# Where four accumulated rows are added over the partitions: one-column products at two places, or row products in column groups at one

## The chip, the cores and the metric

One core of a Trainium2 chip runs the kernel. The metric is the device time of one execution in microseconds (us). Everything the kernel reads lies in the device's main memory (HBM) at its start, and the result is written there.

## The reference, cut to what matters

The block works on 256 latent tokens and 256 context tokens of width 2048. A conditioning vector c is turned into six modulation rows of 2048 numbers, two for the mixing layer's input (shift sh1, scale sc1) and four that are used later:

```python
mod = silu(c) @ w_mod + b_mod                       # 2048 x 12288
sh1, sc1, g1, sh2, sc2, g2 = split(mod, 6)
h  = rms_norm(x, norm_mix_pre) * (1 + sc1) + sh1    # also hc from ctx, c_ctx
y  = hybrid_mixer(h, hc, w_in, ...)                 # projections, 4+4 heads, w_up, w_out
x1 = x + g1 * rms_norm(y, norm_mix_post)
h2 = rms_norm(x1, norm_ffn_pre) * (1 + sc2) + sh2
y2 = (silu(h2 @ ffn_w_gate) * (h2 @ ffn_w_up)) @ ffn_w_down
out = x1 + g2 * rms_norm(y2, norm_ffn_post)
```

The change is about the four later rows g1, sh2, sc2 and g2, each a product of the vector silu(c) with a 2048 x 2048 part of `w_mod`.

## The kernel before

All large products stream a weight matrix through TensorE. A **slot** is 256 rows x 512 columns of weights (512 KB). SyncE's queue loads it into one of eight buffers `raw`; ScalarE rounds it to `w_hi` (L593); VectorE makes the rest `w_lo` (L932); TensorE multiplies hi x hi, hi x lo and lo x hi with the activations as stationary operands (L1344, L1348, L1356, function `products`). ScalarE and VectorE may be up to four slots ahead of TensorE. The stages follow one another in one stream of slots: opening, context blocks, latent blocks (`S_LAT`), up (`S_UP`), out (`S_OUT`), feed-forward (`S_FFN`), down (`S_DOWN`). One slot of the latent blocks is 12 products of 512 columns.

**Step numbers.** The smaller work is written out by hand between slots. In the first seven latent blocks, step p stands behind slot p - 4 on TensorE and ahead of the rounding of slot p on ScalarE and VectorE (the three functions `at_pre`; block t, slot j call `at_pre(8t+j+4)` on TensorE and `at_pre(8t+j)` on the two others). So step 37 on TensorE comes after slot 33 and step 46 after slot 42. From block 6 on, `at_head` and `head_pass` do the same for the heads' work.

**The four rows.** In the context blocks and the first latent blocks VectorE adds up `acc[:, g, :] += wm * silu(c)` (L944), where each `wm` is 128 rows of `w_mod`. This leaves for each of the four rows g 128 partial sums, one in each partition, that have still to be added over the partitions. `add_partitions` (L1487) does that with products whose stationary operand is a 128 x 128 piece of `acc` and whose moving operand is one column of ones: 16 fp32 products for one row, each of which the trace shows as two records. The result stands in columns (channel in the partition).

- At step 37 TensorE adds row 0 (g1). VectorE makes the gate's weight from it at step 39 (`gate_weight`, L1043), TensorE turns it into 16 rows of 128 at step 40 (L1497), ScalarE copies it out at step 43 (L756) and GpSimd stores it to `gwd` (L438).
- Rows 1 to 3 wait: GpSimd stores them to memory when the last accumulation is done (`accd`, 3 MB, L420), ahead of the load of the table `dist` (1 MB, L421), and loads them back as `acc2` while w_out's products run (L559).
- At **the bridge** between out and feed-forward, TensorE adds rows 1 to 3 (L1685 to L1688) and then runs `turn_h2` (L1670, products at L1680), which scales and transposes the new residual `hs` into the feed-forward's input; it needs `diag` (L1287), which holds the reciprocal norms. VectorE makes `mod2`, the shift and scale (L1278, L1281), ScalarE applies it (L893, L896), VectorE makes the low part (L1306), and the products of the feed-forward follow pair by pair.
- The gate's weight for g2 is made at L1288, turned after the 11th slot of the first feed-forward block (L1706), copied at L908 and stored at L569.

**GpSimd's order around the change.** L420 and L421 are issued once the last accumulation is done. Then GpSimd works through the decay tables for four heads, three instructions each (L430, L432, L435), which need `dist`; after that it stores `gwd` (L438), adds decays (L442), loads the first head's operands (L446), and turns the first head's queries and keys with the rotary tables (L481 to L485). TensorE needs these at L1565. ScalarE's steps 40, 42, 44 and 46 need one head's decay table each.

## Time and profile before

| | us |
|---|---|
| median of 3 runs | 1807.98 |
| the three runs | 1805.08, 1808.60, 1807.98 |
| the profiled execution, its time | 1805.67 |
| the profiled execution, its span | 1803.7 |
| TensorE busy with matmuls | 1755.7 (97%) |
| VectorE, ScalarE, GpSimd busy | 976.8, 725.6, 163.5 |

The span is what the profile records from the first to the last instruction; the time holds 2 us around it. Times inside the trace are us from the span's start. TensorE's row is busy nearly throughout, which for matmuls that are pipelined does not say that it runs at its peak: a stretch can be full of records and still be slow, because the products are tiny or because the clock granted to TensorE (PEclk, 1.00 is 2.4 GHz and 0.50 is 1.2 GHz) is at the lower level. Columns of each view are explained where its rows stand.

### The profile page before, as it was taken

What the parts mean: (1) busy time and instruction counts of PE and PEld (TensorE: products, weight loads), DVE (VectorE), ACT (ScalarE), POOL (GpSimd) and SP (SyncE); (2) the same over time, 40 slices, a digit from 0 to 9 for tenths busy, and PEclk for the clock granted to TensorE, in tenths of its full rate; (3) what the DMA queues carried; (4) which work ended last, traced back from release to release, by engine and by line L of the source; (5) the groups of instructions that cost most, each with busy time, mean ns of one, the idle gap of its engine ahead of it and who ended that gap; (6) DMA issues with size and microseconds to landing.
All of it is one profiled execution on the core that took longest, in us unless ns stands there. A gap on an engine that the chain in (4) does not pass through costs nothing.

```text
span 1803.7 us, 21863 instructions
## 1 busy us (share of the span) xinstructions
PE 1755.7 (97%) x8012; PEld 1420.2 (79%) x8012; DVE 976.8 (54%) x1036; ACT 725.6 (40%) x797; POOL 163.5 (9%) x177
## 2 busy tenths in 40 slices
PE   5889999999999999999999999999999999999997
PEld 2448888887788888888888898888888888888886
DVE  2327666655676766676565544444444444444444
ACT  3213222224545543554544454444444444443442
POOL 2000000000007452440000000000000000000000
PEclk8999999999999999999999989999999999999999
DMA  8999988886898766665778636666666666766662
GB/s 312 339 362 354 314 306 310 317 292 249 288 335 295 257 183 206 182 191 159 237 227 329 197 118 203 192 187 188 189 191 188 188 189 190 259 189 193 191 192 76
DMA packets 182283, 422.12 MB, mean 234 GB/s; under 512 B 12816, under 2 KB 13120, under 8 KB 171600
## 3 DMA queue, kind: packets, MB, share of 16 engines
q1 hardware_dynamic: 156288, 304.14, 53.2%
q10 hardware_dynamic: 17856, 82.43, 12.5%
q0 software_dynamic: 8080, 34.75, 5.7%
q8 instruction: 39, 0.64, 0.1%
q14 instruction: 20, 0.16, 0.0%
HBM read 397.66 MB, written 23.61 MB: 234 GB/s over the span
## 4 chain that ended last, share of the span: by engine, by line
PE 93%; ACT 2%; DMA 2%; DVE 2%; issue 1%; SPq 0%; POOL 0%; DVEq 0%; ACTq 0%; POOLq 0%
PE ps L1344 28%; PE ps L1348 28%; PE ps L1356 28%; PE ps L1397 2%; DMA raw<-in_w_mod 1%; PE ps L1490 1%; PE ps L1583 1%; DMA xn<-in_x 1%; PE ps L1599 1%; PE ps L1637 1%; ACT w_hi L593 1%; PE ps L1680 0%; PE ps L1469 0%; PE ps L1554 0%; PE ps L1532 0%
## 5 line engine op out<-in xcount | busy, mean ns | idle before, releaser
L932 DVE TENSOR_TENSOR w_lo<-raw,w_hi 128x1024 fp32r<-128x1024 f32 x496 | 617.2, 1248 | 543.9 <-ACT w_hi L593 541.9
L593 ACT ACTIVATE w_hi<-raw 128x1024 fp32r<-128x1024 f32 x496 | 524.3, 1059 | 838.3 <-PE ps L1356 833.8
L1344 PE MATMUL ps<-w_hi,h_hi 128*128 128x512 f32 x1536 | 485.0, 397 | 7.0 <-ACT w_hi L672 7.0
L1348 PE MATMUL ps<-w_hi,h_lo 128*128 128x512 f32 x1536 | 476.5, 391 | 0.0
L1356 PE MATMUL ps<-w_lo,h_hi 128*128 128x512 f32 x1536 | 421.5, 390 | 0.0
L1344 PEld LDWEIGHTS ps<-w_hi,h_hi 128*128 128x128 f32 x1536 | 285.1, 188 | 70.5 <-issue 13.4
L1348 PEld LDWEIGHTS ps<-w_hi,h_lo 128*128 128x128 f32 x1536 | 289.1, 188 | 61.9
L1356 PEld LDWEIGHTS ps<-w_lo,h_hi 128*128 128x128 f32 x1536 | 288.5, 188 | 61.1 <-DVE w_lo L932 0.2
L944 DVE SCALAR_TENSOR_TENSOR acc<-wm,csil,acc 128x2048 f32<-128x2048 f32 (+1 forms) x60 | 141.0, 2350 | 101.0 <-DMA wm<-in_w_mod 100.9
L1348 PE MATMUL ps<-w_hi,hid_lo 128*128 128x512 f32 x352 | 109.4, 392 | 0.0
L1344 PE MATMUL ps<-w_hi,hid_hi 128*128 128x512 f32 x352 | 109.0, 391 | 0.0
L1356 PE MATMUL ps<-w_lo,hid_hi 128*128 128x512 f32 x352 | 94.9, 391 | 0.0
L1356 PEld LDWEIGHTS ps<-w_lo,hid_hi 128*128 128x128 f32 x352 | 66.1, 188 | 14.7
L1344 PEld LDWEIGHTS ps<-w_hi,hid_hi 128*128 128x128 f32 x352 | 66.0, 188 | 14.5
L1348 PEld LDWEIGHTS ps<-w_hi,hid_lo 128*128 128x128 f32 x352 | 66.1, 188 | 14.1
L1348 PE MATMUL ps<-w_hi,hc_lo 128*128 128x512 f32 x224 | 70.4, 396 | 0.0
L1344 PE MATMUL ps<-w_hi,hc_hi 128*128 128x512 f32 x224 | 70.2, 395 | 0.0
L1356 PE MATMUL ps<-w_lo,hc_hi 128*128 128x512 f32 x224 | 69.9, 393 | 0.0
L1397 PE MATMUL ps<-raw,c_pad 128*32 128x512 f32 x256 | 52.3, 636 | 7.3 <-DMA raw<-in_w_mod 6.0
L1348 PEld LDWEIGHTS ps<-w_hi,hc_lo 128*128 128x128 f32 x224 | 42.5, 190 | 10.1
L1344 PEld LDWEIGHTS ps<-w_hi,hc_hi 128*128 128x128 f32 x224 | 42.3, 189 | 9.7
L1356 PEld LDWEIGHTS ps<-w_lo,hc_hi 128*128 128x128 f32 x224 | 42.1, 188 | 9.8
(254 smaller groups left out, 1174.9 us busy)
## 6 DMA issues: line engine op xcount, KB each, us to landing
raw<-in_w_in SPq DMA_DIRECT2D x176, 512.0 KB, 5.5
wm<-in_w_mod ACTq DMA_DIRECT2D x64, 1024.0 KB, 6.9
raw<-in_ffn_w_gate SPq DMA_DIRECT2D x88, 512.0 KB, 4.5
raw<-in_ffn_w_up SPq DMA_DIRECT2D x88, 512.0 KB, 4.4
raw<-in_ffn_w_down SPq DMA_DIRECT2D x88, 512.0 KB, 4.7
raw<-in_w_mod SPq DMA_DIRECT2D x64, 512.0 KB, 8.2
raw<-in_w_out SPq DMA_DIRECT2D x32, 512.0 KB, 5.2
px<-stage ACTq DMA_DIRECT2D x44, 256.0 KB, 6.3
```

Source lines behind the costliest of these rows:

```text
L593: act.activation(w_hi[:, j % SPLIT, :, :], raw[:, j % RAW, :, :], ACT.Copy).then_inc(w_high, 1)
L932: dve.tensor_tensor(w_lo[:, j % SPLIT, :, :], raw[:, j % RAW, :, :], w_hi[:, j % SPLIT, :, :].bitcast(F32), ALU.subtract).then_inc(w_low, 1)
L944: dve.scalar_tensor_tensor(out=a, in0=wm[:, b, :], scalar=csil[:, k:k + 1], in1=a, op0=ALU.mult, op1=ALU.add).then_inc(S("wm_used"), 1)
L1344: pe.matmul(o, hi[:, kk, c], w_hi[:, q, e, :], start=kk == 0, stop=False)
L1348: pe.matmul(o, lo[:, kk, c], w_hi[:, q, e, :], start=False, stop=False)
L1356: last = pe.matmul(o, hi[:, kk, c], w_lo[:, q, e, :], start=False, stop=kk == last_k)
L1397: last = pe.matmul(bank(4 + n % 2)[g * GROUP:(g + 1) * GROUP, :], c_pad[:, k, :], raw[:, place % RAW, e, :], start=k < 3, stop=k >= KT - 3 ...
L1490: last = pe.matmul(dst[:, first + k:first + k + 1], sums[:, g, k * P:(k + 1) * P], ones[:, :], start=True, stop=True)
L1583: last = pe.matmul(bank(4, 2)[:, a * L:(a + 1) * L], r_kt[:, 2 * (a // 2) + f, (a % 2) * P:(a % 2 + 1) * P], r_qt[:, f, :], start=f == 0, ...
L1599: last = pe.matmul(bank(4)[:, m * RDK:(m + 1) * RDK], r_a[:, a, m * P:(m + 1) * P], r_v[:, a, :], start=a == 0, stop=a == 3)
L1637: last = pe.transpose(bank(4, 2)[:, q * L + m * P:q * L + (m + 1) * P], src[:, m, q * P:(q + 1) * P], ident[:, :])
```

## The change

All four rows are added over the partitions at one place, in the latent blocks, with the operands' parts exchanged: the stationary operand is a 128 x 32 block of ones and the moving operand is 512 columns of `acc`. Each such product gives the sums of 512 channels as a row (the same row in 32 partitions). Product c uses the array's column group c mod 3, so that three run side by side. 12 of the 16 stand at step 37 and 4 at step 40. ScalarE copies the rows out at steps 38 and 41; GpSimd stores them to `sumd` (three DMAs, one for each column group, each from one partition), waits, and loads them back as 64 rows of 128 into `rows`; TensorE turns these at step 46; VectorE makes both gate weights and `mod2` at step 47; TensorE turns both gate weights at step 49, ScalarE copies them and GpSimd stores them to `gwd`, now just ahead of the heads' loop. The detour `accd` and `acc2`, the sums at the bridge and the turn in the feed-forward go.

```diff
     gwd = nc.dram_tensor("gwd", (2, D), F32, kind="Internal").ap()
-    accd = nc.dram_tensor("accd", (3, P, D), F32, kind="Internal").ap()
+    sumd = nc.dram_tensor("sumd", (6, 3, N), F32, kind="Internal").ap()
     hsd = nc.dram_tensor("hsd", (L, D), F32, kind="Internal").ap()
...
         ident = keep("ident", [P, P])
-        ones = keep("ones", [P, 1])
+        ones = keep("ones", [P, GROUP])
         rope = keep("rope", [P, 2, MT, P])
...
         gw_cols = keep("gw_cols", [P, 2, KT])
-        gw_rows = keep("gw_rows", [KT, P])
+        gw_rows = keep("gw_rows", [2 * KT, P])
         csil = keep("csil", [P, 2 * KT])
...
         la = reg("la", [P, 2, 4, GH * GDK], 32)
+        sum_row = reg("sum_row", [3 * GROUP, 6, N], 32)
         cum = reg("cum", [P, 2, GH, L + 1], 48)
...
         y = reg("y", [P, MT, D], 52)
-        acc2 = reg("acc2", [P, 3, D], 69)
         hs = reg("hs", [P, MT, D], 0)
...
             pool.wait_ge(S("wm_used"), 4 * KT)
-            pool.dma_start(accd.rearrange("g p n -> p g n"), acc[:, 1:4, :]).then_inc(S("acc_stored"), 16)
             pool.dma_start(dist[:, :, :, :], k_dist).then_inc(S("dist_landed"), 16)
...
                     .then_inc(S("dist_sum"), 1)
-            pool.wait_ge(S("gw_rows_ready"), 1)
-            pool.dma_start(gwd[0].rearrange("(r q) -> r q", q=P), gw_rows[:, :]).then_inc(S("gw_stored"), 16)
+            pool.wait_ge(S("sum_rows_ready"), 2)
+            for g in range(3):
+                pool.dma_start(sumd[:, g:g + 1, :].rearrange("b g n -> g b n"), sum_row[g * GROUP:g * GROUP + 1, :, :])\
+                    .then_inc(S("sums_stored"), 16)
+            pool.wait_ge(S("sums_stored"), 16 * 3)
+            pool.dma_start(rows[0:4 * KT, :], sumd.rearrange("b g (r q) -> (b g r) q", q=P)[0:4 * KT, :])\
+                .then_inc(S("sums_stored"), 16)
...
                 pool.wait_ge(stored[b], 16 * blocks)
-            pool.wait_ge(S("acc_stored"), 16)
             load_g_qk(0)
...
             add_ctx_decay(RH - 1)
+            pool.wait_ge(S("sum_rows_ready"), 3)
+            pool.dma_start(gwd.rearrange("a (r q) -> (a r) q", q=P), gw_rows[:, :]).then_inc(S("gw_stored"), 16)
             pool.wait_ge(S("gw_stored"), 16)
...
             pool.dma_start(g1w[:, :], gwd[0:1, :].broadcast_to([P, D])).then_inc(S("res_landed"), 16)
-            pool.dma_start(acc2[:, :, :], accd.rearrange("g p n -> p g n")).then_inc(S("acc_landed"), 16)
             pool.wait_ge(S("ssy_ready"), 2)
...
-            pool.wait_ge(S("gw_rows_ready"), 2)
-            pool.dma_start(gwd[1].rearrange("(r q) -> r q", q=P), gw_rows[:, :]).then_inc(S("gw_stored"), 16)
-            pool.wait_ge(S("gw_stored"), 32)
             pool.wait_ge(S("hs_stored"), 16 * MT)
...
                                    scale=1.0 / GATE_NORM).then_inc(S("kw_exp"), 1)
-                if p == 43:
-                    act.wait_ge(S("gw_turned"), 1)
-                    act.activation(gw_rows[:, :], bank(5)[0:KT, 0:P], ACT.Copy).then_inc(S("gw_rows_ready"), 1)
+                if p in (38, 41):
+                    r = (p - 38) // 3
+                    act.wait_ge(S("sums_done"), r + 3)
+                    act.activation(sum_row[:, 4 * r:4 + 2 * r, :],
+                                   bank(4, 4 - 2 * r)[0:3 * GROUP, :].rearrange("p (b n) -> p b n", n=N), ACT.Copy)\
+                        .then_inc(S("sum_rows_ready"), 1)
+                if p == 49:
+                    act.wait_ge(S("sums_turned"), 2)
+                    act.activation(gw_rows[:, :], bank(5)[0:2 * KT, 0:P], ACT.Copy).then_inc(S("sum_rows_ready"), 1)
                 if p in (40, 42, 44, 46):
...
                             .then_inc(S("silu_ready"), 1)
-                    if prev is None and j == 15:
-                        act.wait_ge(S("gw_turned"), 2)
-                        act.wait_ge(S("gw_stored"), 16)
-                        act.activation(gw_rows[:, :], bank(6)[0:KT, 0:P], ACT.Copy).then_inc(S("gw_rows_ready"), 1)
                     if prev is not None or j >= 4:
...
                     dve.tensor_tensor(kw[:, d, :, :], kw[:, d, :, :], gkc[:, :, :], ALU.mult).then_inc(S("kw_ready"), 1)
-                if p == 39:
-                    gate_weight(0, bank(4), 1)
-
-            def gate_weight(d, src, done):
-
-                dve.wait_ge(S("partitions_added"), done)
-                dve.tensor_tensor(gw_cols[:, d, :], src[:, 0:KT], cols2[:, 48 * d:48 * d + KT], ALU.add)\
-                    .then_inc(S("mod2_part"), 1)
-                dve.wait_ge(S("mod2_part"), 1 + 4 * d)
-                dve.tensor_tensor(gw_cols[:, d, :], gw_cols[:, d, :], cols2[:, (4 + d) * KT:(5 + d) * KT], ALU.mult)\
-                    .then_inc(S("mod2_part"), 1)
+                if p == 47:
+                    sums = bank(4)[:, 0:4 * KT]
+                    dve.wait_ge(S("sums_turned"), 1)
+                    dve.tensor_tensor(gw_cols[:, 0, :], sums[:, 0:KT], cols2[:, 0:KT], ALU.add).then_inc(S("mod2_part"), 1)
+                    dve.tensor_tensor(gw_cols[:, 1, :], sums[:, 3 * KT:4 * KT], cols2[:, 3 * KT:4 * KT], ALU.add)\
+                        .then_inc(S("mod2_part"), 1)
+                    dve.tensor_tensor(mod2[:, :, :], sums[:, KT:3 * KT].rearrange("p (a k) -> p a k", a=2),
+                                      cols2[:, KT:3 * KT].rearrange("p (a k) -> p a k", a=2), ALU.add)\
+                        .then_inc(S("mod2_part"), 1)
+                    dve.wait_ge(S("mod2_part"), 3)
+                    for d in range(2):
+                        dve.tensor_tensor(gw_cols[:, d, :], gw_cols[:, d, :], cols2[:, (4 + d) * KT:(5 + d) * KT], ALU.mult)\
+                            .then_inc(S("mod2_part"), 1)
+                    dve.scalar_tensor_tensor(out=mod2[:, 1, :], in0=mod2[:, 1, :], scalar=1.0, in1=cols[:, 3 * KT:4 * KT],
+                                             op0=ALU.add, op1=ALU.mult).then_inc(S("mod2_part"), 1)
...
                                          op0=ALU.mult, op1=ALU.add).then_inc(S("hs_ready"), 1)
-            dve.wait_ge(S("partitions_added"), 3)
-            dve.tensor_tensor(mod2[:, :, :], bank(6)[:, 0:2 * KT].rearrange("p (a k) -> p a k", a=2),
-                              cols2[:, KT:3 * KT].rearrange("p (a k) -> p a k", a=2), ALU.add).then_inc(S("mod2_part"), 1)
-            dve.wait_ge(S("mod2_part"), 3)
-            dve.scalar_tensor_tensor(out=mod2[:, 1, :], in0=mod2[:, 1, :], scalar=1.0, in1=cols[:, 3 * KT:4 * KT],
-                                     op0=ALU.add, op1=ALU.mult).then_inc(S("mod2_part"), 1)
             dve.wait_ge(S("square"), 4 + MT)
...
                 dve.tensor_scalar(diag[:, m, :], ident[:, :], rstd[:, 2 + m:3 + m], None, ALU.mult).then_inc(S("diag_ready"), 1)
-            gate_weight(1, bank(7), 4)
...
                     last.then_inc(S("ctx_sums_done"), 1)
-                if p == 37:
-                    pe.wait_ge(S("wm_used"), 4 * KT)
-                    pe.wait_ge(S("kw_exp"), 2)
-                    add_partitions(acc, 0, bank(4), 0)
-                if p == 40:
-                    turn_gate_weight(0, bank(5))
-
-            def add_partitions(sums, g, dst, first):
-
-                for k in range(KT):
-                    last = pe.matmul(dst[:, first + k:first + k + 1], sums[:, g, k * P:(k + 1) * P], ones[:, :],
-                                     start=True, stop=True)
-                last.then_inc(S("partitions_added"), 1)
-
-            def turn_gate_weight(d, dst):
-
-                pe.wait_ge(S("mod2_part"), 2 + 4 * d)
-                pe.transpose(dst[0:KT, 0:P], gw_cols[:, d, :], ident[:, :]).then_inc(S("gw_turned"), 1)
+                if p in (37, 40):
+                    if p == 37:
+                        pe.wait_ge(S("wm_used"), 4 * KT)
+                        pe.wait_ge(S("kw_exp"), 2)
+                    else:
+                        pe.wait_ge(S("sum_rows_ready"), 1)
+                    for c in range(0, 12) if p == 37 else range(12, 16):
+                        g = c % 3
+                        last = pe.matmul(bank(4 + c // 3 % 4)[g * GROUP:(g + 1) * GROUP, :], ones[:, :],
+                                         acc[:, c // 4, c % 4 * N:(c % 4 + 1) * N], start=True, stop=True,
+                                         tile_position=(0, g * GROUP))
+                    last.then_inc(S("sums_done"), 1)
+                if p == 46:
+                    pe.wait_ge(S("sums_stored"), 16 * 4)
+                    pe.wait_ge(S("sum_rows_ready"), 2)
+                    pe.transpose(bank(4)[:, 0:4 * KT], rows[0:4 * KT, :], ident[0:4 * KT, 0:4 * KT])\
+                        .then_inc(S("sums_turned"), 1)
+                if p == 49:
+                    pe.wait_ge(S("mod2_part"), 6)
+                    pe.transpose(bank(5)[0:2 * KT, 0:P], gw_cols[:, :, :].rearrange("p d k -> p (d k)"), ident[:, :])\
+                        .then_inc(S("sums_turned"), 1)
...
                 if t == 6:
-                    pe.wait_ge(S("gw_rows_ready"), 1)
+                    pe.wait_ge(S("sum_rows_ready"), 3)
                 lat_block(S_LAT + 8 * t, 0, t, lambda j: at_head(0, j - 4) if t == 6 and j >= 4 else at_pre(8 * t + j + 4))
...
                     pe.wait_ge(S("diag_ready"), MT)
-                if j == 3:
-                    pe.wait_ge(S("mod2_part"), 5)
                 if j >= 4:
...
-            pe.wait_ge(S("acc_landed"), 16)
-            add_partitions(acc2, 0, bank(6), 0)
-            add_partitions(acc2, 1, bank(6), KT)
-            add_partitions(acc2, 2, bank(7), 0)
             for j in range(3):
...
                             turn_h2(j + 3)
-                        if prev is None and g == 1 and j == 2:
-                            pe.wait_ge(S("h2_hi_ready"), 8)
-                            turn_gate_weight(1, bank(6))
                         if prev is not None and g == 0 and j == 2:
...
             ffn_block(S_FFN, 0, None)
```

## Rows read from the trace of the kernel before

**Rows 1.** The page, part 4: shares of the chain that ended last, by engine.
```profile
PE 93%; ACT 2%; DMA 2%; DVE 2%; issue 1%; SPq 0%; POOL 0%; DVEq 0%; ACTq 0%; POOLq 0%
```

**Rows 2.** Timeline at the bridge: start, length, engine, line, operation, tiles, records [idle before].
```profile
1036.52 15.60 PE L1490 MATMUL ps<-ones,acc 128*128 128x1 f32 x96
...
1048.44 0.48 DVE L1287 TENSOR_SCALAR diag<-ident,rstd 128x128 f32<-128x128 f32 x2 [0.82 <-POOL rstd L566]
...
1051.98 4.61 PE L1680 MATMUL ps<-diag,hs 128*128 128x128 f32 x24
...
1054.08 1.02 ACT L893 ACTIVATE h2f<-ps,mod 128x256 f32<-128x256 f32 x2 [6.67 <-PE ps L1680]
...
1056.58 0.70 PE L1344 MATMUL ps<-w_hi,h_hi 128*128 128x512 f32 x2
```

**Rows 3.** Busy time by stretch, then granted clock, DMA share and GB/s.
```profile
80.00:100.00 20.00, 18.28 (x101) 8.44 (x99) 6.06 (x13) 3.84 (x6) 0.00 (x0) 1.00 0.93 323
543.00:547.20 4.20, 4.20 (x14) 3.33 (x14) 0.00 (x0) 0.00 (x0) 0.00 (x0) 0.59 1.02 411
1044.00:1048.00 4.00, 4.00 (x21) 4.00 (x20) 1.87 (x4) 3.15 (x4) 0.85 (x3) 0.50 0.87 356
1053.50:1056.50 3.00, 3.00 (x19) 2.90 (x18) 0.69 (x1) 2.39 (x5) 0.00 (x0) 0.66 0.00 0
```

**Rows 4.** Timeline of TensorE in the latent blocks, from step 37 on.
```profile
539.51 3.63 PE L1490 MATMUL ps<-ones,acc 128*128 128x1 f32 x32
543.00 0.76 PE L1344 MATMUL ps<-w_hi,h_hi 128*128 128x512 f32 x2
...
547.41 0.61 PE L1344 MATMUL ps<-w_hi,h_hi 128*128 128x512 f32 x2
...
550.13 0.61 PE L1344 MATMUL ps<-w_hi,h_hi 128*128 128x512 f32 x2
...
552.85 0.27 PE L1497 MATMUL ps<-ident,gw_cols 128*16 128x128 f32 x1
...
555.72 0.62 PE L1344 MATMUL ps<-w_hi,h_hi 128*128 128x512 f32 x2
```

**Rows 5.** Timeline of TensorE in the opening: fp32 products in three column groups.
```profile
66.06 1.90 PE L1397 MATMUL ps<-raw,c_pad 128*32 128x512 f32 x8
...
68.88 3.63 PE L1397 MATMUL ps<-raw,c_pad 128*32 128x512 f32 x24
```

**Rows 6.** Timeline of GpSimd (POOL), from the store of acc to the first head.
```profile
532.13 0.75 POOL L420 DMA_DIRECT2D accd<-acc  x1 [34.17 <-DVE acc L944]
532.88 0.57 POOL L421 DMA_DIRECT2D dist<-in_k_dist  x1
...
549.21 2.22 POOL L430 TENSOR_SCALAR d_tmp<-dist,lg 128x512 f32<-128x512 f32 x1 [15.00 <-issue]
...
569.23 1.29 POOL L435 TENSOR_TENSOR dmat<-dmat,d_tmp 128x512 f32<-128x512 f32 x1
...
596.75 1.30 POOL L442 TENSOR_TENSOR dmat<-dmat,d_ctx 128x512 f32<-128x512 f32 x1
...
612.01 1.72 POOL L485 TENSOR_TENSOR r_k<-r_tmp 128x256 f32<-128x256 f32 x1
```

**Rows 7.** DMA queues from 530 to 545 us: packets, MB, share of the 16 engines.
```profile
q0 software_dynamic: 461, 3.65, 65.0%
q1 hardware_dynamic: 572, 1.12, 19.6%
```

**Rows 8.** DMA issues, whole span: times issued, KB each, median us from issue to landing.
```profile
hsd<-hs POOLq DMA_DIRECT2D x2, 1024.0 KB, 4.8
...
g1w<-gwd POOLq DMA_DIRECT2D x1, 1024.0 KB, 13.3
...
gwd<-gw_rows POOLq DMA_DIRECT2D x2, 8.0 KB, 3.4
```

**Rows 9.** Timeline of TensorE where the change's new waits come.
```profile
569.32 0.62 PE L1344 MATMUL ps<-w_hi,h_hi 128*128 128x512 f32 x2
...
617.84 0.60 PE L1565 MATMUL ps<-ident,r_q 128*128 128x128 f32 x4
```

## The prediction

> **What bounds the kernel now.** I read the chain that ended last first: 93% of it is TensorE's own work, so time is won or lost only where TensorE gets or loses microseconds [rows 1]. The second view is the timeline at the two places that the change touches; the reader is to see there what TensorE does while it is "busy". The third is the granted clock of the same stretches, because a stretch full of records can run at half rate. The last are GpSimd's timeline and the DMA views, because the change makes TensorE wait for a chain that runs through GpSimd and memory.
>
> At the bridge TensorE runs 96 records of one-column products for 15.6 us, from 1036.52 to 1052.1, and only then the products that turn the residual (24 records from 1051.98) [rows 2]. What these need besides TensorE, `diag`, is there at 1048.44 + 0.48 = 1048.92 [rows 2]. So the one-column products end the wait last, but by 3 us only; the other 12 of the 15.6 us lie beside the norm of the residual on the other engines, which the change leaves as it is. The big number, 15.6 us removed, isn't the gain.
>
> **The bridge.** Afterwards the turn starts at about 1049.1 (a product follows its last operand by some 0.1 us), against 1051.98: **-2.9**. What is late next is the chain `diag`, turn, ScalarE, VectorE, first product, which is 1056.58 - 1051.98 = 4.6 us long [rows 2] and moves as a whole. The small VectorE instructions for `mod2` lay inside ScalarE's squares and cost nothing before or after. Against the gain speaks the clock: TensorE will be empty for 12 us ahead of the turn. But the row shows 0.50, the lower level, from 1044 to 1048 while TensorE was full of one-column products, and 0.66 from 1053.5 to 1056.5, in the middle of the turn [rows 3]. The price of a cold start is thus in the 4.6 us already. The Trainium skill, "TensorE: Matmul & The Clock Gate", section "Why this matters for your kernels", advises to leave no idle gaps between bursts of matmuls, since the clock falls back to half; by that rule alone the change gives something back at the bridge. The trace disagrees for this place: busy with one-column products is as cold as empty would be. What is open is how soon the clock comes back after the turn starts. If it comes back one slot later, that slot costs what the cold one in the latent blocks cost, 4.41 instead of 2.72 us, so 1.7 of the 2.9 would go [rows 4]. Bounds of this part: -2.9 and -1.2; I take -2.9, since the turn's own work is the same and starts as cold.
>
> **The latent blocks, removed.** The 32 records at step 37 hold the next slot back by 543.00 - 539.51 = 3.49 us, and this slot then runs 547.41 - 543.00 = 4.41 us where the next takes 2.72 (550.13 - 547.41) [rows 4]; its granted clock is 0.59 [rows 3]. So they cost 3.5 + 1.7 = 5.2. The turn of the gate's weight (L1497) makes its slot 555.72 - 552.85 = 2.87, that is 0.15 over 2.72 [rows 4]. The second turn, in the feed-forward, is the same instruction; I give it 0.15 too. Removed: 5.2 + 0.15 + 0.15 = **-5.5**.
>
> **The latent blocks, added.** The new products have never run with `acc`, but the opening has the same form: fp32, 32 stationary columns, 512 moving ones, three column groups, two records to a product. 24 records (12 products) take 3.63 us and 8 records (4 products) 1.90 us [rows 5]. With 0.1 us for the change of form on either side, steps 37 and 40 cost 3.8 + 2.05 = 5.85. Their clock: a stretch of the opening with such products among others has 1.00 [rows 3], so I expect no cold slot behind them; if there is one, it costs 1.7. Two turns (64 and 32 rows) at 0.15 to 0.3 make 0.45. Added: **+6.3**, between 6.0 and 8.0. ScalarE's two copies and VectorE's six small instructions stand where both engines are up to four slots ahead of TensorE and idle more than a microsecond in each slot; they cost nothing as long as TensorE isn't waiting for them.
>
> **The new wait on TensorE (step 46).** TensorE stands behind slot 42 until 64 rows are back from memory; everything behind it on TensorE, the whole stream of slots, is queued there. Before, the slot after it began at 569.32 [rows 9]. After: step 37 at 539.51 + 3.8 = 543.3, three slots to 551.5, step 40 to 553.5, six slots to **569.9**. The chain it waits for runs on GpSimd: `dist` lands, four heads of decay tables, three stores, a landing, one load, a landing. The tables took 569.23 + 1.29 - 549.21 = 21.3 us [rows 6]. The stores are from one partition, 12 KB each, and no row shows such; the nearest is the 8 KB store of `gwd` with 3.4 us from issue to landing [rows 8]. I take 3.4 for the last store, 1.2 for the two issued ahead of it, and 3.4 for the load: 8.0 after the tables. Five us for each landing, the half again that a busy memory may cost, would make it 11.2.
>
> When does `dist` land? Before, 16.3 us after its issue, since the 3 MB of `accd` went ahead of it in the same queue (issues at 532.13 and 532.88, first use at 549.21) [rows 6]. With `accd` gone it is issued at 532.13. Other transfers of 1 MB from GpSimd's queue landed after 4.8 us (`hsd`) and, behind another of 2 MB, 13.3 us (`g1w`) [rows 8]. In this very stretch GpSimd's queue, with its long packets, moved 3.65 MB while SyncE's moved 1.12 [rows 7]: it isn't pushed aside by the weights. So I take the near end, 5.2 us: 537.3. Tables done at 558.6, rows back at 558.6 + 8.0 = **566.6**, 3.3 us before TensorE asks. Wait: 0, with 3.3 us of cover. ScalarE's copy of step 41 comes after step 40's products, at about 554.5, well before GpSimd wants it.
>
> **The new wait on GpSimd.** `gwd` is now stored ahead of the heads' loop. Behind this wait on GpSimd stand the rotary products of head 0, and TensorE waits for these at L1565. Before, GpSimd was free at 596.75 + 1.30 = 598.05 and had the keys turned at 612.01 + 1.72 = 613.73; TensorE came at 617.84 [rows 6, 9], so 4.1 us of cover. The store takes 3.4 to 3.8 until it lands, which puts the end at 617.1 to 617.5; TensorE comes 0.9 later than before (569.9 - 569.3 and the two turns). Cost: 0, with about 1 us of cover left. This is the thinnest cover of the change.
>
> **The sum.** -2.9 - 5.5 + 6.3 = **-2.1**. The 6 MB less of traffic gain nothing: TensorE waited for no weights where they ran. Against the profiled execution's own 1805.67 that is 1803.6; against the median of the runs, 1807.98, it is 1805.9. The middle of all four executions shown is 1806.8; from it the change gives **1804.7**, which I predict. A measurement of this kernel can tell about 0.2%, 3.6 us, from no change.
>
> **The rivals.** (a) **GpSimd's chain is late at step 46**: `dist` still lands late, because the burst of weight loads that starts at the same moment takes the memory. Place: TensorE behind slot 42. From `dist` to the rows it is 21.3 + 8.0 = 29.3 us, so the wait begins when `dist` lands after 540.6, eats the whole gain when it lands after 542.7, and makes the kernel slower by more than 0.2% after 546.3. At the old landing of 549.2 the rows come at 578.5, the wait is 8.6, and with a cold slot (1.7) behind so long a gap the time is 1804.7 + 8.6 + 1.7 = 1815. For it: the DMA engines are near full around 540. Against: the share in rows 7. Small form (1 to 4 us of wait, 1806 to 1809): 13%; large form (1810 to 1815): 9%. (b) **The cold start lasts longer at the bridge**, or a cold slot follows the new products: +1.7, so 1806.4. For it: TensorE is wholly empty for 12 us. Against: 0.50 is the lower level already. 14%. (c) **The keys of head 0 are late** by one or two us: 1806. For it: 1 us of cover. Against: TensorE's own delay moves with it. 9%. (d) **The change gives more than the sum**: the turn at the bridge warms up sooner than before, and the new products hide their change of form; bridge -4.2, added +6.0, so -3.7 and 1803.1; this needs a start of the turn that happens to lie well to the clock's rise. 10%. (e) The change doesn't do what it says, since the sums aren't what was late: then only +0.8 in the latent blocks stays and 1807.6. Against: the turn begins within 0.1 us of the one-column products' end. 2%. The forecast itself: 43%.
>
> **How the numbers follow.** The forecast's own range is 1802.5 to 1806.8 (the parts' bounds, and the 3.5 us by which equal runs differ, half to a side). To hold 8 in 10 the range takes in (b), (c), (d) and the small form of (a): **1801.8 to 1809.3**. What is left out is the large form of (a) and the runs' tails. Faster by over 0.2%: most of (d) and a third of the forecast, 0.22. Slower: the large form of (a) and a quarter of the small one, 0.13. Same: 0.65.
>
> **What would show each step.** The bridge: first turn record about 0.2 us after `diag`, an empty stretch of 12 us before it, first feed-forward product about 5.2 us after `diag` begins. Latent blocks: 24 records in 3.6 to 3.7 us, the next slot at 2.8 and not 4.4 us. `dist` landing 5 us after issue, first table instruction near 537.5. No TensorE gap behind slot 42, none at L1565. The prediction is wrong if `dist` lands later than 540.6, if a landing of the sums takes over 5 us, or if the first feed-forward slot runs at the lower clock.

## The result and the profile after

The changed kernel takes **1793.72 us** (median of 6 runs, 1792.71 to 1799.03) against 1807.95 for the kernel before beside it (6 runs, 1804.28 to 1812.23): ratio 0.9933, 95% interval 0.992 to 0.9946. That is 14 us faster, where the prediction said 2 (1804.7) and a range from 1801.8 to 1809.3.

The page of the changed kernel: span, busy time of TensorE, and the chain that ended last by engine.

```profile
span 1791.5 us, 21671 instructions
...
PE 1729.5 (97%) x7916; PEld 1398.9 (78%) x7916; DVE 971.5 (54%) x1036; ACT 728.4 (41%) x798; POOL 162.8 (9%) x178
...
PE 92%; DMA 2%; ACT 2%; DVE 2%; issue 1%; SPq 0%; POOL 0%; ACTq 0%; DVEq 0%; POOLq 0%
```

TensorE is still the bound. The two traces laid side by side, cut at the same TensorE records (the first of a stage's own products, or the last turn of a stage's results), say where the 12.2 us of span went:

| stage (us) | before | after | difference |
|---|---|---|---|
| opening, to the last L1375 | 132.96 | 131.79 | -1.17 |
| context blocks, to the first gate product (L1448 before) | 285.08 | 279.48 | **-5.60** |
| gate products and latent blocks, to step 37 | 121.47 | 121.44 | -0.03 |
| step 37 to head 0's first turn | 57.02 | 58.04 | +1.02 |
| heads | 247.71 | 247.69 | -0.02 |
| up, to the last turn of `mg` | 113.28 | 112.43 | **-0.85** |
| out and bridge, to the first turn of `hs` | 94.47 | 91.49 | -2.98 |
| to the first turn of the hidden columns | 61.20 | 60.96 | -0.24 |
| feed-forward, to the last turn of `hid_n` | 445.11 | 445.06 | -0.05 |
| down | 245.31 | 243.04 | **-2.27** |

The edit is in the rows "step 37 to head 0's first turn" and "out and bridge", and there the sizes are those predicted (+0.95 and -2.9). The other 8.7 us (bold) are in three stages in which the diff touches no instruction. The opening scatters by more than its difference: 129.85 to 136.10 over twelve profiled executions of this case's full kernels.

TensorE is busy for every microsecond of the bold stages in both kernels, at full clock, up to the last product of down (behind it come some 12 us in which the result is scaled and stored). So its pace must differ. Busy time by stretch shows it (stretch, length, busy time and matmul records, granted clock, DMA share, GB/s), first in the kernel before:

```profile
150.00:250.00 100.00, 100.00 (x434) 1.00 0.90 320
...
850.00:920.00 70.00, 70.00 (x316) 1.00 0.73 233
1150.00:1450.00 300.00, 300.00 (x1353) 1.00 0.65 189
1580.00:1780.00 200.00, 200.00 (x876) 1.00 0.57 177
```

and in the changed one:

```profile
150.00:250.00 100.00, 100.00 (x443) 1.00 0.92 328
...
850.00:920.00 70.00, 70.00 (x319) 1.00 0.73 235
1150.00:1450.00 300.00, 300.00 (x1349) 1.00 0.65 189
1580.00:1780.00 200.00, 199.87 (x882) 1.00 0.55 168
```

The same time holds more products in the context blocks, up and down, and not in the feed-forward (the last row of the changed kernel ends 0.13 us behind its last product). From start to start of two 128x512 products it is 231.2 ns on average in the context blocks and 228.9 to 229.0 ns in up and down before, and **226.7 to 226.8 ns** in these stages after; out and feed-forward had 226.7 to 226.8 already, and the latent blocks' undisturbed slots 2.72 us, so 226.7 ns a product, too. The 1056 products of down (88 slots of 12) by 2.2 ns are the 2.3 us of its row.

The stages that gained have one thing in common: they have stationary operands (`hc_hi` and `hc_lo`, `o_hi` and `o_lo`, `hid_hi` and `hid_lo`) in the region of overlaid tiles that `reg` gives out, while the latent blocks, out and feed-forward use `h_hi` and `h_lo` alone, which lie ahead of it. In up and down all products have such operands. In the context blocks only half have: there two products with `h_hi` or `h_lo` and two with `hc_hi` or `hc_lo` take turns. The region starts behind the tiles of `keep`, rounded up to 64 bytes. `ones` went from 4 bytes in a partition to 128, and the region moved from byte 133696 to 133760 of each partition (worked out from the sizes of the tiles ahead of it).

**The edit's own places.** The bridge afterwards, timeline of all engines (start, length, engine, line, operation, tiles, records, idle before):

```profile
1041.82 0.48 DVE L1288 TENSOR_SCALAR diag<-ident,rstd 128x128 f32<-128x128 f32 x2 [0.83 <-POOL rstd L570]
...
1042.36 4.55 PE L1681 MATMUL ps<-diag,hs 128*128 128x128 f32 x24 [12.29 <-DVE diag L1288]
...
1046.98 0.70 PE L1344 MATMUL ps<-w_hi,h_hi 128*128 128x512 f32 x2
```

The turn starts 0.06 us after `diag`; from there to the first product it is 4.62 us, against 4.60 before [rows 2]. The clock of that stretch:

```profile
1030.00:1042.00 12.00, 0.07 (x1) 0.00 (x0) 7.64 (x8) 6.32 (x9) 2.52 (x4) 0.59 0.66 235
1042.00:1044.00 2.00, 1.64 (x7) 1.65 (x8) 0.30 (x2) 0.00 (x0) 0.00 (x0) 0.50 0.50 205
1044.00:1047.00 3.00, 2.93 (x20) 2.77 (x18) 0.69 (x1) 2.50 (x5) 0.00 (x0) 0.71 0.00 0
1047.00:1050.00 3.00, 3.00 (x14) 2.49 (x15) 1.34 (x2) 2.25 (x5) 0.00 (x0) 1.00 0.00 0
```

TensorE in the latent blocks: the sums of steps 37 and 40, the turns of steps 46 and 49, head 0's rotary operands.

```profile
532.71 3.63 PE L1488 MATMUL ps<-acc,ones 128*32 128x512 f32 x24
...
544.66 1.90 PE L1488 MATMUL ps<-acc,ones 128*32 128x512 f32 x8
...
563.08 0.27 PE L1495 MATMUL ps<-ident,rows 64*128 64x64 f32 x1
...
571.58 0.27 PE L1499 MATMUL ps<-ident,gw_cols 128*32 128x128 f32 x1
...
611.99 0.60 PE L1568 MATMUL ps<-ident,r_q 128*128 128x128 f32 x4
```

GpSimd's chain between them:

```profile
525.12 0.57 POOL L420 DMA_DIRECT2D dist<-in_k_dist  x1 [34.02 <-DVE acc L947]
...
530.52 1.56 POOL L429 TENSOR_SCALAR d_tmp<-dist,lg 128x512 f32<-128x512 f32 x1 [4.45 <-issue]
...
551.58 1.54 POOL L434 TENSOR_TENSOR dmat<-dmat,d_tmp 128x512 f32<-128x512 f32 x1
553.06 1.62 POOL L438 DMA_DIRECT2D sumd<-sum_row  x3
557.80 0.55 POOL L441 DMA_DIRECT2D rows<-sumd  x1 [3.12 <-DMA sumd<-sum_row]
...
589.53 0.55 POOL L535 DMA_DIRECT2D gwd<-gw_rows  x1
592.76 3.19 POOL L485 TENSOR_TENSOR r_tmp<-r_q,rope 128x256 f32<-128x256 f32 x4 [2.69 <-DMA gwd<-gw_rows]
...
606.39 1.73 POOL L489 TENSOR_TENSOR r_k<-r_tmp 128x256 f32<-128x256 f32 x1
```

and the DMA issues (times issued, KB each, us from issue to landing):

```profile
dist<-in_k_dist POOLq DMA_DIRECT2D x1, 1024.0 KB, 5.2
...
sumd<-sum_row POOLq DMA_DIRECT2D x3, 12.0 KB, 2.8
rows<-sumd POOLq DMA_DIRECT2D x1, 32.0 KB, 4.8
```

No idle time stands before any of TensorE's five rows: none of the new waits is felt. The granted clock is 1.00 from 532 to 548 us, so no cold slot follows the new products.

### The profile page after: what moved, and what is told of

Its sections match the earlier page's. It is cut to its first block, busy times and chain, and to the rows that moved or that the text cites. A ratio compares the mean times of both kernels' runs of the same rounds, so it can differ in the third digit from the quotient of the medians.

```text
span 1791.5 us, 21671 instructions
## 1 busy us (share of the span) xinstructions
PE 1729.5 (97%) x7916; PEld 1398.9 (78%) x7916; DVE 971.5 (54%) x1036; ACT 728.4 (41%) x798; POOL 162.8 (9%) x178
## 4 chain that ended last, share of the span: by engine, by line
PE 92%; DMA 2%; ACT 2%; DVE 2%; issue 1%; SPq 0%; POOL 0%; ACTq 0%; DVEq 0%; POOLq 0%
PE ps L1344 28%; PE ps L1348 28%; PE ps L1356 28%; PE ps L1397 1%; DMA raw<-in_w_mod 1%; PE ps L1586 1%; DMA xn<-in_x 1%; PE ps L1602 1%; PE ps L1640 1%; ACT w_hi L594 1%; PE ps L1681 1%; PE ps L1469 0%; PE ps L1557 0%; PE ps L1535 0%; PE ps L1460 0%
```

## The experiments

**Theory A**: the 8.7 us come from the place of the stationary operands. **Rival B**: they come from the 6 MB less of traffic through memory or from something else that the moved sums do to the run of engines. **Rival C**, for the part at the bridge: the one-column products cost by their form and the clock, wherever they stand.

### The wide tile of ones alone

```diff
-        ones = keep("ones", [P, 1])
+        ones = keep("ones", [P, GROUP])
...
-                    last = pe.matmul(dst[:, first + k:first + k + 1], sums[:, g, k * P:(k + 1) * P], ones[:, :],
+                    last = pe.matmul(dst[:, first + k:first + k + 1], sums[:, g, k * P:(k + 1) * P], ones[:, 0:1],
```

> The kernel before with one edit: the tile of ones is allotted 32 columns instead of 1, and its first column is used. All work is as before; the tiles allotted after it move up by 96 bytes, and the region of the large tiles (context activations, merged heads, hidden activations) moves from an address that is 64 modulo 128 to one that is 0 modulo 128. Theory A (placement): the 10 us that the prediction didn't have come from where stationary operands lie, so the context blocks, the up stage and the down stage speed up as in the changed kernel and nothing else does: 1797 to 1799. Theory B (the work itself: less traffic and other timing make TensorE's pace better): no change, 1806 to 1809.

Measured: 1797.34 us (4 runs), ratio 0.9939 (0.9919 to 0.9959). Context blocks 279.48, up 112.43, down 243.06 us: to 0.02 us the stages of the changed kernel, with the sums, the detour and all traffic as before. Of the 8.7 us nothing is left for rival B to explain.

### The region moved by itself

In each kernel only the start of the region is changed, by 64 or 128 bytes:

```diff
-        base = (cursor[0] + 63) // 64 * 64
+        base = (cursor[0] + 63) // 64 * 64 + 64
```

> The kernel before with the region of the large tiles moved up by 64 bytes (0 modulo 128) and no other tile moved. Theory A in its narrow form (the large region alone): 1797 to 1799, equal to the kernel with the wide tile of ones. If the small tiles that lie between (rotary tables, masks, columns) carry part of the gain, it stays above that kernel. Theory B: 1806 to 1809.

Measured: 1798.48 us (4 runs), 0.9948 (0.993 to 0.9965); context 279.48, up 112.47, down 243.06. The edit of `ones` isn't needed, nor does it matter where the small tiles lie; the place of the region is enough.

> The changed kernel with the region of the large tiles moved up by 64 bytes, so that it lies at 64 modulo 128 as in the kernel before; the small tiles stay where the change puts them. Theory A (placement of the large region): it loses the 10 us again and keeps the 2 us of the moved sums, 1803 to 1806. Theory B (the work itself): as the changed kernel, 1793 to 1796.

Measured: 1809.36 us (10 runs), 1.001 (1.0 to 1.0019). The changed kernel loses its whole gain by 64 bytes more, and more than I expected (1803 to 1806), since I took the address modulo 128 for the rule: context 285.62, up 114.94, down 249.76. The same stretches as above:

```profile
150.00:250.00 100.00, 100.00 (x433) 1.00 0.88 318
...
850.00:920.00 70.00, 70.00 (x312) 1.00 0.71 228
...
1580.00:1780.00 200.00, 200.00 (x859) 1.00 0.56 177
```

Down is slower here than in the kernel before (859 records against 876): 233.3 ns a product.

> The kernel before with the region of the large tiles moved up by 128 bytes, so that it is still 64 modulo 128. Theory A with the address modulo 128 as its rule: as before, 1806 to 1809. A theory in which any move shifts a chance coincidence between tiles would let this one differ as much as the move by 64 bytes. Theory B: 1806 to 1809.

Measured: 1815.62 us (10 runs), 1.0046 (1.0034 to 1.0059); context 285.62, up 114.94, down 249.81, so the stages of the last one: both have the region at 192 modulo 256. By the rule modulo 128 it should have stayed at 1806 to 1809: that a step of 128 bytes changes these stages ends that rule. Between these two kernels, equal in placement and measured in the same rounds, the moved sums make 6.3 us.

> The changed kernel with the region of the large tiles moved up by 128 bytes. In the changed kernel it lies at 128 modulo 256, here at 0 modulo 256; both are 0 modulo 128. If the address modulo 128 alone sets the pace: 1793 to 1796, 226.7 ns a product in context, up and down stages. In the kernel before the move from 64 to 192 modulo 256 cost 8.8 us, so 128 isn't the whole period; if the period is 256, this place may be better or worse than 128: up to 10 us either way.

Measured: 1810.28 us (8 runs), 1.0024 (1.0012 to 1.0035); context 286.66, up 114.55, down 248.90. Region at 0 modulo 256: slow too, where the rule modulo 128 said 1793 to 1796. Of four places only one, 128 modulo 256, is good, and it is where `w_hi` (byte 49280), the moving operand, also stands modulo 256; so do `w_lo`, `h_hi` and `h_lo`.

### One stage's operand alone

```diff
-        hid_hi = reg("hid_hi", [P, FF_BLOCKS * 4, L], 0, F32R)
-        hid_lo = reg("hid_lo", [P, FF_BLOCKS * 4, L], 44, F32R)
+        hid_hi = at("hid_hi", [P, FF_BLOCKS * 4, L], F32R, base + 64)
+        hid_lo = at("hid_lo", [P, FF_BLOCKS * 4, L], F32R, base + 44 * K + 64)
```

(and the two small tiles behind them, so that nothing overlaps.)

> The kernel before with only the hidden activations (hid_hi, hid_lo, hid_n, and junk2 that shares hid_n's place) moved up by 64 bytes, so that the down stage alone has its stationary operands at 0 modulo 128. Theory A (TensorE's pace is set by the address of the stationary operand): the down stage takes 243.0 us instead of 245.3 and its products start 226.7 ns apart instead of 228.9; context blocks 285 us and up stage 113.3 us stay. In all 2.3 us less than the kernel before, within what single runs scatter. Rival (the whole layout or the position of another tile sets the pace): the down stage stays at 245.3.

Measured: 1802.68 us (one run). Context 285.09, up 113.28 as before; down 243.04:

```profile
150.00:250.00 100.00, 100.00 (x434) 1.00 0.90 318
...
1580.00:1780.00 200.00, 200.00 (x884) 1.00 0.57 176
```

Only the stage whose stationary operand was moved changes its pace, as expected. It isn't the start of the region that matters, nor the tiles that stayed.

### TensorE alone, over the addresses

A kernel that computes nothing of the reference: TensorE runs groups of 36 products (128x128 stationary, 512 columns moving) and from group to group one operand starts 32 or 64 bytes further on.

> Not the block: a kernel that leaves the whole computation out and only measures TensorE. It runs 88 groups of 36 products (128 x 128 stationary, 128 x 512 moving, rounded fp32), the stationary operand's address going through 0 to 992 by 32 bytes with the moving operand at 0, then 0 to 448 by 64 for each place of the moving operand from 64 to 448. Groups lie on two lines in turn. Theory A1 (the pace depends on where the stationary operand lies against the moving one): the groups with equal residues modulo 256 run at 226.7 ns from start to start, others at 228 to 234, and the fast place moves along with the moving operand. Theory A2 (the stationary address alone decides): the same places are fast for every place of the moving operand. If neighbouring engines or the DMA are needed for the effect, all groups run alike, at about 216 or 227 ns.

Timeline of TensorE; the rows alternate between two source lines, one row a group. Moving operand at 0, stationary at 0, 32, 64, 96, 128, 160, 192 and 224:

```profile
20.50 8.33 PE L47 MATMUL ps<-mov,stat 128*128 128x512 f32 x36
28.67 8.55 PE L49 MATMUL ps<-mov,stat 128*128 128x512 f32 x36
37.06 8.56 PE L47 MATMUL ps<-mov,stat 128*128 128x512 f32 x36
45.46 8.59 PE L49 MATMUL ps<-mov,stat 128*128 128x512 f32 x36
53.88 8.53 PE L47 MATMUL ps<-mov,stat 128*128 128x512 f32 x36
62.26 8.55 PE L49 MATMUL ps<-mov,stat 128*128 128x512 f32 x36
70.65 8.40 PE L47 MATMUL ps<-mov,stat 128*128 128x512 f32 x36
78.89 8.56 PE L49 MATMUL ps<-mov,stat 128*128 128x512 f32 x36
```

From one start to the next: 8.17, 8.39, 8.40, 8.42, 8.38, 8.39, 8.24 us. Over the last 25 products of each group, ns from start to start:

| moving \ stationary, modulo 256 | 0 | 64 | 128 | 192 |
|---|---|---|---|---|
| 0 | **226.7** | 233.4 | 232.4 | 228.9 |
| 64 | 228.8 | **226.6** | 233.4 | 232.2 |
| 128 | 232.1 | 228.8 | **226.7** | 233.4 |
| 192 | 233.3 | 232.2 | 228.9 | **226.6** |

The stationary offsets from 256 to 1023, and the moving ones from 256 to 448, repeat these to 0.3 ns. So the pace depends on the **difference** of the two addresses modulo 256, and up and down of the full kernels fit: stationary minus moving is 192 before (228.9 to 229.0), 0 after (226.7 to 226.8), 64 in the two kernels with the region at 192 (233.3), 128 with the region at 0 (232.4; 232.1 to 232.5 in the scan). From 20 to 750 us the granted clock is 1.00, ScalarE, VectorE and GpSimd are idle and the DMA queues as good as idle (1 GB/s), so the difference needs none of them.

> Again only TensorE and none of the block's computation. 12 groups move the stationary operand by 4 to 28 and by -16 to -4 bytes against the fast place; 10 change the pattern (one stationary tile for all products, one PSUM bank for all, two banks, another moving tile for each product, the kernel's own order) at offset 0 and at offset 64; 12 shorten the moving operand to 480, 448 and 384 columns at offsets 0, 64, 128 and 192. If the two reads meet in time and place (theory A1), the fast place is narrow or wide by some tens of bytes, the pattern changes nothing beyond 1 ns, and with fewer columns the groups fall by 13 to 14 ns for 32 columns while the differences between the offsets stay. If the effect belonged to PSUM banks, the one-bank group would stand out.

Averages over the last 27 intervals from start to start in each group:

| stationary offset, 512 columns | 0 | 4 | 8 | 12 | 16 | 20 | 24 | 28 | 240 | 244 | 248 | 252 |
|---|---|---|---|---|---|---|---|---|---|---|---|---|
| ns a product | **226.7** | 232.4 | 230.8 | 230.2 | 233.3 | 233.3 | 231.1 | 235.0 | 228.3 | 233.3 | 233.3 | **226.7** |

Of the offsets tried next to 0, only 0 and 252 are fast: the fast place is narrow. One stationary tile or twelve in turn, one bank or four, the moving tile changed at each product or at every fourth: 226.7 at offset 0 and 233.4 at offset 64 in all ten groups. What does matter is the number of moving columns; I had expected the differences between the offsets to stay. Timeline of the groups with 480 columns (stationary at 0, 64, 128 and 192):

```profile
203.34 7.97 PE L51 MATMUL ps<-mov,stat 128*128 128x480 f32 x36
211.15 7.94 PE L53 MATMUL ps<-mov,stat 128*128 128x480 f32 x36
218.92 7.85 PE L51 MATMUL ps<-mov,stat 128*128 128x480 f32 x36
226.61 8.02 PE L53 MATMUL ps<-mov,stat 128*128 128x480 f32 x36
```

At 480 columns the best of the four offsets is 128 (213.3 ns; 216.5, 215.9 and 218.2 at 0, 64 and 192), at 448 it is 192 (200.0; 202.6, 202.2 and 203.7 at 0, 64 and 128), at 384 both 0 and 192 (173.3; 176.7 and 175.9 at 64 and 128). So "the same place modulo 256" is shown as a rule for 512 columns of rounded fp32 only. Since the length of a product matters, it may be about how the loads of the next stationary operand meet the reads of the moving one in time; that is argued, not shown.

### The sums by their form

The changed kernel with all four rows as one-column products at step 37, and with neither stores nor loads of the sums:

```diff
-                if p in (37, 40):
...
+                    for c in range(4 * KT):
+                        last = pe.matmul(bank(4)[:, c:c + 1], acc[:, c // KT, c % KT * P:(c % KT + 1) * P], ones[:, 0:1],
+                                         start=True, stop=True)
```

> The changed kernel with all four rows added at step 37 in the old form: 64 one-column products (128 records) with 128 stationary columns of acc, whose sums stand in columns at once, so that the row copies, the detour through memory and the first turn go. It prices the form of the products apart from their place. From the rows of before (117 ns a record in the latent blocks, where the clock holds for most of 32 records, 160 to 190 at the bridge): 128 records hold TensorE for 15 to 20 us, against 5.8 for the 16 row products, and a cold slot or two come behind: 10 to 16 us slower than the changed kernel, 1804 to 1810. A theory in which the form doesn't matter and only the place does: 1794 to 1796.

Measured: 1815.02 us (3 runs), 1.0042 (1.0021 to 1.0063), some 20 us above the changed kernel and above the 1804 to 1810 that I expected. TensorE there, and after it the clock:

```profile
533.30 24.80 PE L1471 MATMUL ps<-ones,acc 128*128 128x1 f32 x128
...
557.95 1.20 PE L1331 MATMUL ps<-w_hi,h_hi 128*128 128x512 f32 x2
```

```profile
540.00:556.00 16.00, 16.00 (x76) 16.00 (x77) 0.00 (x0) 0.00 (x0) 10.21 (x8) 0.50 0.11 43
```

128 records hold the next slot back by 24.65 us, or 193 ns each, against 3.49 us for 32, or 109 ns each, in the kernel before [rows 4]. From start to start such a record takes 112 ns while the granted clock is 1.00 and 213 ns while it is 0.50. In all seven strings of such records that the traces of the kernels with one-column sums hold and that are longer than 32, the clock fell 2.2 to 5.3 us after the string's start and stayed down to its end: the longer the string is, the more of it runs at 0.50. At the same placement this is 17.7 us above the kernel whose columns are split between the two places (1797.34, in other rounds; 18.6 by the two ratios). So moved in the old form the sums lose, and the new form is what makes the move a gain; theory C holds. Whether row products at the bridge would have gained as much wasn't run.

### The bridge kept busy

50 products of 512 columns, whose result isn't read, are put where TensorE is empty:

```diff
+            for j in range(FILL):
+                pe.matmul(bank(7), h_lo[:, j % KT, 0:P], h_hi[:, 2 * (j % 8):2 * (j % 8) + 2, :], start=True, stop=True)
             for j in range(3):
                 turn_h2(j)
```

> The changed kernel with 50 products of 512 columns, whose results nobody reads, issued on TensorE at the bridge ahead of the turn of the residual (11.3 us of work in a wait of 12.3), to hold the clock up. If the cold start of the turn costs what its rows suggest (24 records in 4.55 us against 8 in 1.05 once warm), the turn takes 3.2 us and the feed-forward's first product comes 0.7 to 1.4 us sooner: 1792.3 to 1793. If ScalarE's and VectorE's chain behind the turn sets the first product anyway, no change: 1793.7. Slower if the filling products run past the end of the wait.

Measured: 1793.3 us (4 runs), 0.9928 (0.9911 to 0.9945). The granted clock stays at 1.00 from 1020 to 1050 us. The bridge:

```profile
1028.67 11.49 PE L1688 MATMUL ps<-h_hi,h_lo 128*128 128x512 f32 x50
1041.14 2.94 PE L1682 MATMUL ps<-diag,hs 128*128 128x128 f32 x24 [0.97 <-DVE diag L1289]
1044.84 0.70 PE L1345 MATMUL ps<-w_hi,h_hi 128*128 128x512 f32 x2 [0.76 <-issue]
```

Warm, the turn takes 2.94 us where it took 4.55, and the first product comes 3.70 us after its start, against 4.62. The cold start at the bridge is thus worth **0.9 us**, inside the 0.7 to 1.4 that I expected. ScalarE and VectorE bound the rest: the low part that VectorE makes behind ScalarE's two instructions is ready at 1044.74, 0.10 us before the product. As a total it can't be told from the changed kernel's.

### The two once more, side by side

> The kernel before with `ones` as wide as in the changed kernel, the same edit as in e1_before_wide_ones, beside the changed kernel on the same chip in five rounds: both have their stationary operands at the same addresses, so the difference between the two is what the moved sums themselves give. If the sum of the prediction holds (its terms were -2.9 and +0.8), it is 2.1 us. If the bridge's cost is as large as the stage out and bridge showed over the kernels with one-column sums there (mean 95.7 against 91.5, so 4.2) and the removed cold slot cancels the new products' price, it is about 4. Expected here: 1797.5, 0.994.

> The changed kernel, as given, in the same rounds. Expected 1793.5, 0.992; its runs lie closer together (within 2 us) than those of the kernel with the sums at the bridge (within 4 us or more), if the moment at which the clock falls under the one-column products is what makes equal runs differ there.

Measured: 1799.61 us (6 runs), 0.9955 (0.9941 to 0.9968), and 1795.96 (5 runs), 0.9939 (0.9926 to 0.9952), before 1807.38. At the same placement the moved sums give 3.65 us by the medians, but the intervals of the two ratios overlap: by these runs alone neither the 2.1 of the prediction's sum nor no gain at all is excluded. The stages are plainer: out and bridge is 95.99 us in the first and 91.49 in the second. The runs of the changed kernel didn't lie within 2 us as I expected (5.9 us, against 8.3 for the other); in the two profiled executions much of the difference is the opening, 136.10 and 131.47 us. The one-column products at the bridge of this kernel, and those of the first kernel with the wide tile of ones:

```profile
1035.08 17.12 PE L1490 MATMUL ps<-ones,acc 128*128 128x1 f32 x96
1028.49 18.47 PE L1490 MATMUL ps<-ones,acc 128*128 128x1 f32 x96
```

## Why the prediction was wrong

**The step that failed** is the list of what the change moves. It went through instructions, waits and queues, and costed the widened `ones` at nothing without naming it. The sum then took the pace of all other products as given. The runs showed in its place that the pace of TensorE's products hangs on the place of the stationary operand against the moving one, and that the wider `ones` moved the former. In the trace of before the same products took 231.2 ns from start to start in the context blocks, 228.9 to 229.0 in up and down and 226.7 to 226.8 in the others, and nothing in the prediction asked why. The placement alone gives -5.6, -0.85 and -2.3, so 8.7 us in the profiled execution, and 8 to 11 us by the ratios of the kernels that change nothing but the placement (0.9939, 0.9948, 0.9955). Of the 11.0 us between forecast and result it is most; the sum had no term for it.

**Point by point:**
- The bridge: predicted -2.9 and a start about 0.1 us after `diag`; measured -2.98 and 0.06. The cold start moved as a whole, 4.62 against 4.60 us. The clock fell while TensorE was full of one-column products as well as while it was empty. Rival (b) didn't come.
- But -2.9 rests on one execution. In the six kernels with the sums at the bridge that stage took 94.47, 97.36, 94.62, 97.12, 95.13 and 95.99 us (mean 95.8), and 91.46 to 91.50 in the six with the sums moved. The string of 96 took 15.60 to 18.47 us, and its length decided: the stage less the string is 78.9 us in all six. The length in turn goes with how soon the clock fell: 5.3 us after the string's start in the trace of before, the shortest string, 2.2 us in the longest. The trace of before was thus the luckiest of the six. The mean gain is 4.3 us: the term was **mis-sized** by 1.4, since one profile doesn't show how the length of a stretch at the lower clock scatters.
- Removed at step 37: the cold slot was there before [rows 4] and is gone after; but in the six kernels that have these sums, step 37 to the heads took 57.02 to 57.06 us in four, 55.42 in the one with `hid_hi` moved and 58.61 in the wide `ones` run again. Over the 10 us from step 37 the granted clock was 0.83 in the four, 1.00 in the second and 0.66 in the third: the cold slot's 1.7 can also be nothing or twice as much. The mean is 57.03, so here the one profile happened to show the usual size.
- Added: 3.63 and 1.90 us, as the opening's rows gave [rows 5]; net +1.02 against +0.95. With the bridge's mean, the moved sums give 4.3 - 1.0 = 3.3 us.
- `dist`: 5.2 us to its landing, as taken from the nearer end. Rival (a) fell with it.
- The sums' way through memory: three stores in 1.62 and 3.12 more to the landing, a load of 4.8. Rows back at about 562.6 (557.80 + 4.8), and TensorE turned them at 563.08: the cover was 0.5 us, not 3.3. TensorE came 30.4 us after step 37, as the sum had it (569.9 - 539.51); but the tables took 22.6 us instead of 21.3 (530.52 to 553.12), and from their end to the rows it was 9.5 instead of 8.0. So the wait is 0 as predicted, but the thinnest cover was here and not at head 0's keys.
- Keys of head 0: ready at 608.12 (606.39 + 1.73), TensorE at 611.99, 3.9 us of cover where 1 was predicted: GpSimd was through with the decays 1.6 us sooner, counted from step 37 (56.9 against 58.5 us), and the store cost 3.2 instead of up to 3.8. Rival (c) didn't come.
- The second turn's 0.15, taken out of the feed-forward: that stage with its first slots got shorter by 0.24 + 0.05 us, too little to tell.
- "6 MB less of traffic gain nothing": right. The load of `acc2` ran during w_out's products; from the last turn of `mg` to the last of these products it is 78.78 to 78.81 us in all twelve kernels, with and without it.

The Trainium skill, "TensorE: Matmul & The Clock Gate", section "Step-by-step: what each phase is for", says that loading the next tile's weights doesn't steal read bandwidth from the running matmul. Here 226.7 and 233.4 ns stand for the same products on an otherwise idle core, and the difference hangs on the place of the stationary operand against that of the moving one. These 3% are more than the sentence lets one expect, but no run shows that they are lost at the reads.

**Open** is the mechanism behind the difference modulo 256. Open is also why the context blocks ran at 231.2 ns before: the scan gives 226.7 for the difference of `h_hi` and 228.9 for that of `hc_hi`. There the two kinds take turns in pairs, and the products with `h_hi` slow down too (224 to 236 ns from start to start in the trace of before, where the changed kernel has 226 or 227); the scan kept one difference for a whole group, and a mixed pattern wasn't run. And open is the size of the moved sums' own gain between about 2 and 6 us (3.3 by the mean stages, 3.65 side by side, 6.3 between the two kernels with the region at 192).

## What to carry to other kernels

Whoever changes a tile's size moves every tile behind it: compare the addresses of TensorE's operands before and after, not only the instructions, and count products per 100 us in stages that the edit doesn't touch. For products of 512 moving columns of rounded fp32 place the stationary operand so that its address equals the moving operand's modulo 256; here 64 bytes of padding were worth 8 to 11 us of 1808. For 480 and 448 columns the best place was another, so for other widths it has to be measured. And replace long strings of one-column products by products with the data as the moving operand: the clock fell 2.2 to 5.3 us into them, although TensorE was full.

## What the runs showed of the hardware that was not expected

- The pace of fully pipelined products (rounded fp32, 128x128 stationary, 512 columns moving) depends on stationary minus moving address modulo 256: 226.7 ns at 0, 233.4 at 64, 232.2 at 128, 228.9 at 192, and most offsets that aren't multiples of 64 are slow (230 to 235; 240 has 228.3, 252 has 226.7). The best offset is another for 480 (128) and 448 columns (192).
- The clock fell to 0.50 under one-column fp32 products, with TensorE busy for 16.00 of 16 us: a record takes 112 ns at 1.00 and 213 ns at 0.50, 128 records took 24.80 us, and 96 took 15.60 to 18.47 us by the moment at which the clock fell.
- Filling 12 empty us with products kept the clock at 1.00; the turn behind them got 1.6 us shorter, and the first product came 0.9 us sooner.
